# First attention layer: a split hand-over of results, one wide exponential, reordered modulation, and filler matmuls in the mixture of experts

## What is computed

```python
def nsa_mixer(h, ...):                      # 16 heads of 64, 512 tokens
    ...
    lg = einsum(q_b, kc) * scale + bias     # branch 0: 31 compressed keys
    p_c = masked_softmax(lg, dist_c >= 0)
    o_c = einsum(p_c, vc)
    ...                                     # branches 1 and 2: up to 512 keys
    o = gate_b[..., 0:1] * o_c + gate_b[..., 1:2] * o_s + gate_b[..., 2:3] * o_w
# first_block, for each layer:
    mod = einsum('bd,sde->sbe', silu(c), ada_w[layer]) + ada_b[layer]   # modulation: shift, scale, gate
    y = nsa_mixer(h, ...)                   # layer 0; an HGRN mixer in layer 1
    x = x + gate * y
    h = rms_norm(x, g) * (1 + scale) + shift
    y = hier_moe(h, ...)                    # 16 experts, top 2 of each token
    x = x + gate * y
```

## Time and profile before

| what | value |
|---|---|
| time, median of 3 runs | 4420.54 us (4418.85 to 4424.25) |
| time of the profiled execution | 4425.69 us |
| its span | 4423.9 us |
| TensorE, VectorE, ScalarE busy | 4105.3, 2628.0, 1983.6 us |
| mean granted clock of TensorE | 0.955 of full speed |
| scores of the first unit, last value matmuls of attention | 238.57 us, 535.78 us |
| first projection matmul | 551.43 us |

### The profile page before, as it was taken

How to read it: one execution, slowest core, us unless ns; L and a number is a source line. 1 busy time by engine, 2 the same in 40 slices (tenths; PEclk the granted TensorE clock), 3 DMA queues, 4 the chain that set the end, 5 groups by cost and what they waited for, 6 DMA issues and landing times.

```text
span 4423.9 us, 61005 instructions
## 1 busy us (share of the span) xinstructions
PE 4105.3 (93%) x25436; PEld 3196.4 (72%) x25436; DVE 2628.0 (59%) x4322; ACT 1983.6 (45%) x3374; POOL 167.7 (4%) x151
## 2 busy tenths in 40 slices
PE   7889879998898799979999978999999999789998
PEld 4656568886777688857777756777777776567776
DVE  4456648996437599974445855544544457655444
ACT  3245538885346388853223343322332233433222
POOL 0000010000002100010000000000000000000000
PEclk9999989998999899989999989999999999899999
DMA  5144239996220399962222101222222221012221
GB/s 204 67 177 163 109 140 422 406 409 253 76 77 3 150 424 408 409 233 96 84 85 99 58 2 40 77 96 95 86 95 95 86 100 49 2 40 77 95 95 67
DMA packets 61853, 635.88 MB, mean 144 GB/s; under 512 B 6743, under 2 KB 7127, under 8 KB 27016
## 3 DMA queue, kind: packets, MB, share of 16 engines
q1 hardware_dynamic: 46024, 575.34, 33.1%
q0 software_dynamic: 8928, 32.51, 2.0%
q10 hardware_dynamic: 6624, 24.12, 1.3%
HBM read 601.49 MB, written 30.45 MB: 143 GB/s over the span
## 4 chain that ended last, share of the span: by engine, by line
PE 82%; DVE 10%; ACT 5%; issue 2%; DMA 2%; POOL 0%; POOLq 0%; DVEq 0%; SPq 0%; ACTq 0%
PE ps L357 14%; PE ps L358 14%; PE ps L359 14%; PE ps L1394 4%; PE ps L1396 4%; PE ps L1395 4%; PE ps L1412 2%; PE ps L1414 2%; PE ps L1413 2%; PE ps L1007 2%; DVE wbuf_r L338 2%; PE ps L378 1%; PE ps L1026 1%; PE ps L379 1%; PE ps L568 1%
## 5 line engine op out<-in xcount | busy, mean ns | idle before, releaser
L358 PE MATMUL ps<-arena_r,wbuf_r 128*128 128x512 f32 x2848 | 1139.9, 400 | 0.0
L338 DVE TENSOR_TENSOR wbuf_r<-slot,wbuf_r 128x512 fp32r<-128x512 f32 (+1 forms) x832 | 594.4, 722 | 679.0 <-ACT wbuf_r L328 670.1
L357 PE MATMUL ps<-hT_r,wbuf_r 128*128 128x512 f32 x2080 | 841.9, 405 | 18.2 <-DVE arena_r L470 12.2
L359 PE MATMUL ps<-hT_r,wbuf_r 128*128 128x512 f32 x2080 | 827.9, 398 | 0.0
L328 ACT ACTIVATE wbuf_r<-slot 128x512 fp32r<-128x512 f32 (+1 forms) x832 | 506.3, 614 | 716.2 <-PE ps L359 607.6
L358 PEld LDWEIGHTS ps<-arena_r,wbuf_r 128*128 128x128 f32 x2848 | 537.7, 189 | 134.8 <-issue 4.6
L357 PEld LDWEIGHTS ps<-hT_r,wbuf_r 128*128 128x128 f32 x2080 | 393.4, 189 | 140.7 <-DVE arena_r L470 20.7
L359 PEld LDWEIGHTS ps<-hT_r,wbuf_r 128*128 128x128 f32 x2080 | 393.7, 189 | 98.5
L357 PE MATMUL ps<-arena_r,wbuf_r 128*128 128x512 f32 x768 | 306.7, 399 | 0.0
L359 PE MATMUL ps<-arena_r,wbuf_r 128*128 128x512 f32 x768 | 305.2, 397 | 0.0
L1292 DVE TENSOR_TENSOR wbuf_r<-arena,wbuf_r 128x1024 fp32r<-128x1024 f32 x164 | 195.5, 1219 | 46.1 <-ACT wbuf_r L1285 45.7
(11 more groups left out here) (534 smaller groups left out, 7067.4 us busy)
## 6 DMA issues: line engine op xcount, KB each, us to landing
arena<-in_moe SPq DMA_DIRECT2D x82, 2048.0 KB, 10.8
slot<-in_moe SPq DMA_DIRECT2D x54, 2048.0 KB, 10.9
slot<-in_gu SPq DMA_DIRECT2D x44, 2048.0 KB, 7.4
slot<-in_ada SPq DMA_DIRECT2D x20, 2048.0 KB, 7.7
slot<-in_down SPq DMA_DIRECT2D x16, 2048.0 KB, 7.5
slot<-in_win SPq DMA_DIRECT2D x12, 2048.0 KB, 7.4
yrow<-arena ACTq DMA_DIRECT2D x46, 512.0 KB, 10.5
slot<-in_hgrn SPq DMA_DIRECT2D x8, 2048.0 KB, 7.9
```

Of the source, the lines that this page charges most:

```text
L338: v.tensor_tensor(lo[:, 0:w], src[:, off:off + w], hi[:, 0:w].bitcast(F32), ALU.subtract) \
L357: p.matmul(bank, hi[:, cs], rh[:, k, :], start=k == 0, stop=False, skip_group_check=True)
L358: p.matmul(bank, hi[:, cs], rl[:, k, :], start=False, stop=False, skip_group_check=True)
L359: t = p.matmul(bank, lo[:, cs], rh[:, k, :], start=False, stop=k == kt - 1, skip_group_check=True)
```

## The change

1. Of attention's results: when unit 8 of a tile is done, ACT copies the bank as the rounded high part to `hTr`, and DVE subtracts it from the bank and writes the low part to `att.lo` (in the place of the queries, which that tile no longer needs). Both do it a step later than DVE's copy before. The projection takes these two as its operands; its own eight copies and eight differences are gone. Its first three weight pieces are cut during the last tile of attention. PE waits for each low part by itself and starts the projection's first output tile at once; the edge and `route_early_pe` come behind that tile.
2. Of branch 0: DVE subtracts the maxima (one instruction of 256 columns), ACT takes one exponential of 256 columns without bias and sum, and DVE makes the sums (one reduction).
3. Of the modulation: in each step PE's `extra` stands ahead of the values and works on index s-5, a step sooner. ACT's and DVE's stays at s-6, behind their part of `values`.
4. In both MoE layers: `busy_pe` puts matmuls of a constant with 512 columns, whose results nobody reads, into PE's list: 4 ahead of the ranks, 12 behind DVE's last row and ahead of the first gathered block, 12 ahead of the transposes at the end.
5. In layer 0 the router's input lies in the arena (`m.h`) and no longer in `hT`, which now holds the high part.

```diff
+        def busy_pe(p, bank, count):
+            for _ in range(count):
+                p.matmul(bank, ident, const[:, 0:512], start=True, stop=True, skip_group_check=True)
...
+        att.lo = arena_r[:, 8192:12288].rearrange("p (k t) -> p k t", k=8)
...
-            pipeline(len(att.units), scores, None, None, turn, None, values, lambda u: next(extra, None))
+            def extra_values(u):
+                next(extra, None)
+                values(u)
+            pipeline(len(att.units), scores, None, None, turn, None, extra_values)
...
-                    for i in range(8):
-                        x = pb[:, 0, i * 32:i * 32 + 31]
-                        a.activation(x, x, ACT.Exp, bias=c[:, i:i + 1], accum_out=c[:, 8 + i:9 + i]) \
-                            .then_inc(*act.mark("att", "exp", u))
+                    a.activation(pb[:, 0, 0:256], pb[:, 0, 0:256], ACT.Exp).then_inc(*act.mark("att", "exp", u))
...
+            def values(u):
+                tile, b, qt = att.units[u]
+                if b == 2 and qt == 3:
+                    act.wait_ge(*pe.at("att", "values", u))
+                    a.activation(hTr[:, tile, :], att.out.buf(tile), ACT.Copy).then_inc(*act.mark("att", "o hi", tile))
+                if tile == 7 and b == 2 and qt < 3:
+                    cut_hi(a, cuts, qt)
+            def extra_values(u):
+                values(u)
+                next(extra, None)
+            pipeline(len(att.units), None, exps, None, None, turn, None, extra_values)
...
+                if b == 0:
+                    v.tensor_reduce(c[:, 8:16], pb[:, 0, 0:256].rearrange("p (a b) -> p a b", a=8), AX, ALU.add) \
+                        .then_inc(*dve.mark())
...
                 if b == 2 and qt == 3:
-                    dve.wait_ge(*pe.at("att", "values", u))
-                    v.tensor_copy(hT[:, tile, :], att.out.buf(tile)).then_inc(*dve.mark("att", "out", tile))
-            pipeline(len(att.units), None, bias, scale, None, None, values, lambda u: next(extra, None))
+                    dve.wait_ge(*act.at("att", "o hi", tile))
+                    v.tensor_tensor(att.lo[:, tile, :], att.out.buf(tile), hTr[:, tile, :].bitcast(F32), ALU.subtract) \
+                        .then_inc(*dve.mark("att", "o lo", tile))
...
+            pipeline(len(att.units), None, bias, scale, None, None, None, extra_values)
...
         def res_pe(p, m, moe):
-            edge(pe, m.name)
-            route_early_pe(p, moe)
-            pe.wait_ge(*dve.at(m.name, "o lo", 7))
+            pe.also("edge", m.name)
             pieces = iter(range(16))
             for i in range(8):
...
+                        ready=(lambda k: dve.at("att", "o lo", k)) if i == 0 else None)
+                if i == 0:
+                    for eng in (act, dve):
+                        pe.wait_ge(*eng.at("edge", m.name))
+                    route_early_pe(p, moe)
+                else:
                     route_tile_pe(p, moe, i - 1)
...
+            busy_pe(p, bank, 4)
             pe.wait_ge(*dve.at(n, "chosen"))
...
+                    if b == 0 and hf == 0:
+                        pe.wait_ge(*dve.at(n, "row", 3, 1))
+                        busy_pe(p, bank, 12)
                     pe.wait_ge(*gathered[b % 2].at(n, b))
...
+            busy_pe(p, out[0], 12)
             for t4 in range(4):
                 pe.wait_ge(*dve.at(n, "mixed", t4))
```

48 lines of the change are left out of this document (22 added, 26 removed).

## The result

The changed kernel takes 4379.58 us (median of four executions, 4376.46 to 4384.57), the kernel before 4422.40 beside it (4418.85 to 4431.78): a ratio of 0.9901, 95% interval 0.9881 to 0.9920, some 43 us less. The forecast was 22 less, with a range from 4387 to 4410.

The account below looks back on a forecast made before the run. The prediction took TensorE, 82% of the chain that ended last, as the bound, with DVE 10%. Its terms summed to -21.7 us from 4425.69: 4404.0 profiled, 4398.8 as a median, range 4387 to 4410.

Parts of the forecast that it names:

- The seam: Between attention and projection: first output tile 5.6 us, shift pair 2.6, second tile starts at 546.0 instead of 559.81; -13.9 us.
- Branch 0: Attention's branch 0: one wide exponential removes five 1.18 us waits of PE (-5.9) and shortens the first tile's chain by 1.1; -7.0.
- The old copy and the new wait: Attention steps 4 and 5: seven 0.96 us waits go (-6.7); row-copy waits (+5.4) and a last-tile low-part wait (+2.2) come.
- The clock within attention: Slow matmul stretches in attention cost 1.3 us each, six times; three were taken as gone: -4 us, bounds 0 and -8.
- The rival that the clock gives more: No slow stretches in attention (-4 more), last transposes and layer 0's row sums at the high level (-4 more): 4391, chance 0.12.
- Fillers ahead of the ranks: Four busy matmuls ahead of the ranks delay them, by 2.7 us in layer 0 and 3.9 in layer 1: +6.6.
- Ahead of the first block: Twelve fillers ahead of the first gathered block take 13.3 us and raise its clock: net -1.9 in each layer, -3.8.
- At the end: Twelve fillers in PE's 12.47 us idle time ahead of the last transposes cost nothing and gain -0.5, bounds 0 and -4.
- The rival by which fillers stay at the low clock: Unit-matrix fillers don't raise the clock and run at 1.87 us throughout; kernel 26.7 us slower, 4447, chance 0.04.
- Attention gives nothing: Rival: the wait for the modulation's row, or the clock, takes all that branch 0 and the old copy give; 4409, chance 0.16.

Follow-up runs that it names:

- a_best_start: Changed kernel with the last tile's output in the modulation's bank, no fillers ahead of the ranks, four ahead of attention's first turned matmul: 4371.66 us, ratio 0.9868.
- b_fill: Kernel before plus four busy matmuls ahead of attention's first turned matmul and four ahead of step 5's turned matmuls in each tile: ratio 1.0037.
- a_best: Changed kernel with the last tile's output in the bank the modulation has left and without the four busy matmuls ahead of the ranks: ratio 0.9891.

## Why the forecast was right in its sign and wrong in its size

**The seam** (-13.9): right. 22.05 became 7.94, -14.1. The first output tile took 5.68 (said 5.6), the pair of shift matmuls 2.26 (said 2.6).

**Branch 0** (-7.0): right in place. The waits of 1.18 are gone and the idle time ahead of the first turned matmul fell from 4.77 to 3.56. The wide exponential takes 0.42 (said 0.45), and the copy follows it by 0.32:

```profile
306.34 0.42 ACT L1054 ACTIVATE arena<-arena 128x256 f32<-128x256 f32 x1 [2.86 <-DVE arena L1118]
306.66 0.64 ACT L1070 ACTIVATE arena<-ps 128x256 f32<-128x256 f32 x2
```

**The old copy and the new wait** (-6.7, +5.4, +2.2): right. The first went, L582 waits 5.1 in six tiles, and the last tile's L1028 waits 1.89 (said 2.2). With branch 0 the waits sum to -6.1 in the forecast; PE's idle time fell by 7.1 within attention and by 1.2 ahead of it, 8.3. Most of the difference is in the three copy waits at the start and in the last tile, 3.4 us before and 1.7 after, for which the forecast had nothing.

**The clock within attention** (-4, bounds 0 and -8): this is the step that failed. The mechanism, a level that falls in most tiles, was right; its size was wrong. Busy time fell by 20.2, of which some 18 are the clock by the estimate above, where the term was 4. Two errors are in it. I sized it by one group of twelve matmuls a tile in the six tiles of the earlier trace rows, 1.3 us each, and so left out tile 0, where the same group takes 2.93 us. (The 1.53 that the forecast compares with is a second group of the sixth of these tiles, not of the last tile; that tile's are as fast.) The table by tile gives more: length times what the clock lacks to 1.00 is 8.5 us in tile 0, 1.9 in each of the five next and 3.4 in tile 6, 21 in all. And I took half of the falls as gone by argument, where all went but one in tile 0, and a new one came in tile 7. The bound should have been -21 and not -8, which takes the forecast's lower end, and the range with it, below the time that came. With -18 in place of -4 the sum gives some 4385, within 6 us of the 4379.58. That the falls would go with the three edits was a guess of the forecast and not worked out, and which of them go is not explained by the runs either.

**The rival that the clock gives more** (0.12, 4391) had the direction, and the same short measure: no slow stretches in attention was put at 4 us more.

**Fillers ahead of the ranks** (+6.6): +3.2 and +2.5, so +5.7. **Ahead of the first block** (-3.8): twelve took 13.46 in layer 0 and 13.31 in layer 1 (said 13.3), in layer 0 they ended 0.5 past the time at which the gathered rows were there, and in all they gave back 3.1 and 3.3, -6.4. **At the end** (-0.5): they ended before the first transposes, which took 1.09 in place of 1.94, and the last group took 1.97 as before, so that nothing was gained. All fillers together come to about -1 in these terms where the forecast had +2.3; the ratios, as said, can't confirm this. The rival by which fillers stay at the low clock (4447) is refuted: the first four took 3.60, 0.90 each, with a unit matrix as operand. The Trainium skill's page "TensorE: Matmul & The Clock Gate", Part 1, "What's actually happening", on which that rival's price was weighed, has activity release the throttle, and the trace agrees: these fillers ran at the high level.

**Attention gives nothing** (0.16): the three single runs show how near this was. Alone the parts give 0.3 and 3.6 us in attention and cost 23.6, and it is by the three together that the waits don't replace one another. The forecast had named both covers, the shorter exponential ahead of steps 1 and 7 and the long group ahead of the new tile's first values, and for the waits it was right by its reasons. For the clock its reason, thin matmuls that are spread apart, is neither shown nor refuted.

Of the 49.1 us between the two spans, 41.4 lie between the first turned matmul and the projection's second output tile. The rest isn't shown to be of the change: the repetition of the changed kernel, the same program, ends attention at 506.5 us, 4.9 earlier than the first, and has a span of 4380.3, 5.5 longer, so that some 10 us come and go behind attention without any edit.

## What to carry to other kernels

Before sizing a stall, tabulate the granted clock by stage: length times what it lacks to 1.00 is an upper bound on what a steadier supply of work can give, and here it was more than all the stalls in the list of waits together (21 us against 16). It is a bound only: where PE then waits for another engine, a higher clock gives nothing, as in tile 0 of a_best_start. In a loop that several engines share, look for the chain that each edit shortens and for the one that it lengthens; edits that are worthless or harmful alone (+35 us for one of these) can be worth 30 together, so measure the set, and keep for each wait that you move the name of the work that is to cover it. A filler delays what stands behind it in the engine's list by all of its length that the wait doesn't cover (3.2 of 3.6 us ahead of the ranks), and must write a place that is free before the wait it is to fill.

## What the runs showed of the hardware that was not expected

The granted clock fell to 0.50 for some 3 us at a time, and in tile 0 of the kernel before for 10 (from 253 to 263 us), although PE was 94% busy in the tile around it (35.44 of 37.59 us), and taking waits away could go with more falls: with the wide exponential alone PE's idle time fell from 16.2 to 10.1 us and the clock from 0.93 to 0.91. Busy matmuls ahead of a stretch do lift the clock (tile 0 from 0.78 to 0.96 with eight in b_fill, from 0.92 to 1.00 with four between a_best and a_best_start), but 3.7 us of dense work directly ahead of thin matmuls did not keep it up in four tiles of six, and in a_best_start the lifted clock saved no time. Two profiles with the same program in attention differed by one such fall, 1.4 us.
